# A hybrid encoder block on one core: the router's logits taken from sums ahead of the norm, the 64 greatest found in two halves, the first gather split, and one expert unit placed outside the weight ring

## The reference

```python
proj = h @ w_in                                    # z | xBC | dt | u | gate_a | gate_b
y_a  = ssd_branch(z, xBC, dt)                      # Mamba-2 scan in both directions, 24 heads
y_b  = s5_branch(u)                                # S5 scan in both directions, then GLU
mix  = sigmoid(gate_a) * y_a + sigmoid(gate_b) * y_b
h    = LN(alpha * h + mix @ w_o) * ln1_g + ln1_b
aff  = softmax(h @ w_router, axis=-1)              # 16 experts
gate, idx = top_k(aff.T, 64)                       # each expert takes the 64 tokens it likes best
xin  = h[idx]                                      # (16, 64, 1024)
hid  = silu(xin @ w_e1) * (xin @ w_e3)             # (16, 64, 2816)
moe  = scatter_add(idx, (hid @ w_e2) * gate)
out  = LN(alpha * h + moe) * ln2_g + ln2_b
```

## Time and profile before

| | |
|---|---|
| time, median of 3 runs | 2252.95 us (2252.62 to 2254.93) |
| profiled execution | 2250.3 us, its span 2248.3 us |
| PE busy | 1995.2 us, 89% of the span |
| DVE busy | 674.6 us, 30% |
| ACT busy | 328.2 us, 15% |
| POOL busy | 314.7 us, 14% |
| HBM traffic | 614.39 MB read, 9.78 MB written |

### The profile page before, as it was taken

How to read it: one execution, slowest core, us unless ns; L and a number is a source line. 1 busy time by engine, 2 the same in 40 slices (tenths; PEclk the granted TensorE clock), 3 DMA queues, 4 the chain that set the end, 5 groups by cost and what they waited for, 6 DMA issues and landing times.

```text
span 2248.3 us, 19706 instructions
## 1 busy us (share of the span) xinstructions
PE 1995.2 (89%) x8321; PEld 938.4 (42%) x8321; DVE 674.6 (30%) x1075; ACT 328.2 (15%) x547; POOL 314.7 (14%) x278
## 2 busy tenths in 40 slices
PE   8996899998979999598889889879889888988987
PEld 4664544455554444433334334334334333333332
DVE  6599965589970112300000000000000000000002
ACT  1433212144450001100000000000000000000001
POOL 2866600066640000000000000000000000000001
PEclk9898999999989999699999999999989999999999
DMA  5531221110013218389999999999999999999995
GB/s 138 126 107 26 66 96 69 39 52 28 29 57 131 84 66 351 122 341 427 429 428 424 428 428 425 431 426 427 429 427 427 428 426 427 428 427 426 427 428 228
DMA packets 86887, 625.45 MB, mean 278 GB/s; under 512 B 21036, under 2 KB 34576, under 8 KB 57616
## 3 DMA queue, kind: packets, MB, share of 16 engines
q1 hardware_dynamic: 74400, 616.41, 66.8%
q10 hardware_dynamic: 12400, 7.79, 1.2%
HBM read 614.39 MB, written 9.78 MB: 278 GB/s over the span
## 4 chain that ended last, share of the span: by engine, by line
PE 47%; DMA 28%; DVE 9%; ACT 2%; issue 1%; SPq 0%; DVEq 0%; ACTq 0%
PE ps L843 47%; DMA arena<-in_w_e 28%; ACT arena L568 1%; DVE arena L1598 1%; DVE arena L1546 1%; ACT L568 1%; DVE arena L1602 1%; DVE arena L1573 1%; DVE arena L1603 1%; DVE arena L1571 1%; DVE arena L1599 0%; DVE arena L1590 0%; DVE arena L1678 0%; DVE arena L1595 0%; DVE arena L1689 0%
## 5 line engine op out<-in xcount | busy, mean ns | idle before, releaser
L843 PE MATMUL ps<-arena 128*64 128x512 f32 (+7 forms) x7786 | 1927.6, 534 | 213.8 <-DMA arena<-in_w_e 114.5
L843 PEld LDWEIGHTS ps<-arena 128*64 128x64 f32 (+2 forms) x7786 | 877.4, 164 | 1247.8 <-issue 1062.5
L568 ACT ACTIVATE arena<-ps 128x512 f32<-128x512 f32 (+5 forms) x286 | 161.8, 597 | 1697.3 <-PE ps L843 898.2
L1698 DVE TENSOR_TENSOR arena<-arena,ps 128x512 f32<-128x512 f32 (+1 forms) x48 | 30.3, 645 | 581.5 <-PE ps L843 581.5
L560 POOL TENSOR_TENSOR arena<-arena 128x1024 f32<-128x1024 f32 x3 | 7.1, 2355 | 1324.8 <-ACT arena L568 1324.8
L1707 DVE TENSOR_TENSOR arena<-arena,ps 128x512 f32<-128x512 f32 x48 | 33.1, 690 | 338.5 <-PE ps L843 338.5
L568 ACT ACT_TABLE_LOAD x71 | 91.1, 1283 | 23.8 <-issue 21.4
L568 ACT ACTIVATE arena<-arena 64x512 f32<-64x512 f32 (+6 forms) x138 | 62.8, 513 | 164.2 <-DVE arena L1603 93.5
L1531 DVE SCALAR_TENSOR_TENSOR arena<-arena 128x512 f32<-128x512 f32 x80 | 62.5, 781 | 2.8
L1689 DVE TENSOR_TENSOR arena<-arena 128x512 f32<-128x512 f32 x8 | 5.6, 694 | 182.4 <-PE ps L1260 181.4
L544 POOL TENSOR_TENSOR arena<-arena 128x768 f32<-128x768 f32 x16 | 24.3, 1522 | 171.6 <-PE ps L1004 134.1
(11 more groups left out here) (180 smaller groups left out, 769.7 us busy)
## 6 DMA issues: line engine op xcount, KB each, us to landing
arena<-in_w_e SPq DMA_DIRECT2D x128, 2816.0 KB, 28.9
arena<-in_w_e SPq DMA_DIRECT2D x80, 2048.0 KB, 28.5
arena<-in_w_in SPq DMA_DIRECT2D x9, 2048.0 KB, 8.6
arena<-in_w_e SPq DMA_DIRECT2D x16, 1024.0 KB, 30.6
arena<-in_w_in SPq DMA_DIRECT2D x5, 1536.0 KB, 6.4
arena<-in_w_out_ssd SPq DMA_DIRECT2D x4, 1536.0 KB, 6.7
gate_scratch<-arena ACTq DMA_DIRECT2D x16, 256.0 KB, 2.4
arena<-gate_scratch SPq DMA_DIRECT2D x4, 1024.0 KB, 8.0
```

The source lines that it names most:

```text
L568: return act.activation(out, in_, func, **kw)
L843: return pe.matmul(out, lhsT, rhs, start=a, stop=z)
L1698: tt(o, o, ps[:, i, 0:w], ALU.mult).then_inc(s.hid_ready, 1)
```

## The change

- **Logits from the sums ahead of the norm.** Since h = (s - mean) / deviation * g + b with s = alpha x + mix @ w_o, the logits are (s @ (g w) - mean * sum(g w)) / deviation + sum(b w). So PE transposes `x_res` and multiplies it with the scaled router weights, and DVE corrects the result (`logits(c)`). The transposes and the router's matmuls of chunk c stand inside `out_product(c + 1)`. The scaled weights and the two rows of sums are made early: w_router is loaded behind slice 4 of w_in, POOL scales it twice, and PE and ACT make the two rows (`logit_rows`).
- **The 64 greatest in two halves.** `greatest(0)` works on chunks 0 and 1 between the two halves of the last output product, `greatest(1)` on chunks 2 and 3. The larger of the one's i-th and the other's (65 - i)-th value are the 64 greatest, and the least of them is a threshold. Slot numbers come from comparisons with the threshold and eight matmuls with triangles and ones.
- **The first gather in two parts.** Three of its eight blocks come ahead of `up(0, 0)`, five behind its first group.
- **Unit 7 aside.** It goes into the place of `x_res`, once h is finished (`h_ready` 4), and the ring holds the others. The order of release shifts: unit 8 now takes the place of unit 0.
- ln2_g and ln2_b are loaded behind the first pair's `up` instead of ahead of the search; ln1_g and ln1_b are read once more, as columns, with the early parameters.

The core of the diff:

```diff
@@ ring of expert weights: one unit's place lies outside it @@
-def ring_places(sizes, start, end):
+def ring_places(sizes, start, end, aside):
     for u, n in enumerate(sizes):
+        if u in aside:
+            places.append(aside[u])
+            behind.append(None)
+            continue
+        ASIDE = 7
+        unit_place, unit_behind = ring_places(unit_size, ring_at, WORDS, {ASIDE: aside_at})
@@ SP @@
             slices(0, FIRST_GATE + 1)
+            sp.dma_start(w_r[:, 0], A["w_router"][0].rearrange("(k p) e -> p k e", p=P)).then_inc(s.wr_loaded, 16)
...
-            sp.dma_start(w_r, A["w_router"][0].rearrange("(k p) e -> p k e", p=P)).then_inc(s.wr_loaded, 16)
...
-                if unit_place[u] + n_ > W0 - KT * EXPERTS and unit_behind[u] is None:
+                if u == ASIDE:
+                    sp.wait_ge(s.h_ready, TT)
+                elif unit_place[u] + n_ > W0 - router_words and unit_behind[u] is None:
                     sp.wait_ge(s.wo_ps, 2 * TT)
-                    sp.wait_ge(s.logit_ps, TT)
+                    sp.wait_ge(s.max_ready, TT)
@@ POOL @@
+            pool.wait_ge(s.par_ready, 1)
+            pool.wait_ge(s.wr_loaded, 16)
+            n.link(pool.tensor_tensor(w_r[:, 1], w_r[:, 0], last(ln1_cols[:, 1], EXPERTS), ALU.mult))
+            pool.tensor_tensor(w_r[:, 0], w_r[:, 0], last(ln1_cols[:, 0], EXPERTS), ALU.mult).then_inc(s.wr_scaled, 1)
+
             pool.wait_ge(s.rot_ready, 1)
             powers(fine, 0)
@@ ACT: ln1_g and ln1_b join the early parameters; later @@
+            act.wait_ge(s.rows_ps, 1)
+            n.done(f(logit_rows.rearrange("p r e -> p (r e)"), ps[:, 7, 0:2 * EXPERTS], ACT.Copy))
             act.wait_ge(s.seg_ps, 1)
...
+            for c in range(TT + 1):
+                if c < TT:
+                    mix_transposed(c)
+                if c >= 2:
+                    x_transposed(c - 2)
+                    exponents(c - 2)
+                if c >= 1:
+                    deviation(c - 1)
+            x_transposed(TT - 1)
+            exponents(TT - 1)
...
+                if p == 0:
+                    act.wait_ge(s.up_ps, 12)
+                    for i, name in enumerate(("ln2_g", "ln2_b")):
+                        act.dma_start(lnrow[:, i, :], A[name][0].partition_broadcast(P)).then_inc(s.ln_loaded, 16)
@@ PE @@
+            pe.wait_ge(s.wr_scaled, 1)
+            for k in range(KT):
+                r = mm(ps[:, 7, 0:2 * EXPERTS].rearrange("p (r e) -> p r e", r=2), ones, w_r[:, :, k, :], k == 0, k == KT - 1)
+            r.then_inc(s.rows_ps, 1)
...
+            mm(counts, m_le_l, over, True, False)
+            for c in range(1, TT):
+                mm(counts[:, c:], ones_l, over[:, 0:TT - c], False, False)
             for c in range(TT):
-                r = pe.transpose(ps[:, 4, EXPERTS * c:EXPERTS * c + EXPERTS], cum[:, P * c:P * c + P], ident[0:EXPERTS, 0:EXPERTS])
+                r = mm(counts[:, :, 1, :], ones_l, first(over[:, c, 0, :], TT), False, c == TT - 1)
             r.then_inc(s.slot_ps, 1)
...
                 for j in range(ROW_BLOCKS):
+                    if p == 0 and which == 0 and j == 1:
+                        first_gather(range(3, KT))
+                        pe.wait_ge(s.xin_copied, 2)
@@ DVE @@
+            def greatest(i):
+                dve.wait_ge(s.affT_ps, 2 * i + 2)
+                src = ps[0:EXPERTS, 2, 256 * i:256 * i + 256]
+                for r in range(CAP // 8):
+                    best = top64[:, i, 8 * r:8 * r + 8]
+                    n.link(dve.max(best, src))
+                    if r + 1 < CAP // 8:
+                        n.link(dve.match_replace(work, best, src, -1.0))
+                        src = work
...
             for c in range(TT):
+                residual(c, 0)
+                if c == TT - 1:
+                    greatest(0)
+                if c >= 1:
+                    logits(c - 1)
+                    affinities(c - 1)
+                residual(c, 1)
                 dve.wait_ge(s.wo_read, 2 * c + 2)
                 moments(x_res[:, c, :], c, s.var_ready)
                 dve.wait_ge(s.var_ready, c + 1)
+                deviation_inverse(c)
+                if c == TT - 1:
+                    logits(c)
                 centred(x_res[:, c, :], h[:, c, :], c)
...
+            affinities(TT - 1)
+            greatest(1)
+            n.link(tt(top64[:, 0], top64[:, 0], top64[:, 1, ::-1], ALU.max))
+            dve.tensor_reduce(threshold, top64[:, 0], AX.X, ALU.min).then_inc(s.threshold_ready, 1)
+            dve.wait_ge(s.threshold_ps, 1)
+            limit = first(ps[:, 5, 0:EXPERTS], TT)
+            tt(over[:, :, 0, :], aff, limit, ALU.is_gt).then_inc(s.over_ready, 1)
+            tt(over[:, :, 1, :], aff, limit, ALU.is_equal).then_inc(s.over_ready, 1)
+            normed(h[:, TT - 1, :], TT - 1).then_inc(s.h_ready, 1)
```

More of the change, by code:

```diff
@@ L206, in encoder @@
         ysT = H.take(S5_W // P, SEQ)
-        w_r = H.take(KT, EXPERTS)
+        w_r, logit_rows = H.take(2, KT, EXPERTS), H.take(2, EXPERTS)
         uT = ysT
@@ L295, in encoder @@
         xin = S.take(KT, P)
-        S3 = Space(arena, S.at, mix_end)
-        affT, work, cum = (S3.take(SEQ, parts=EXPERTS) for _ in range(3))
-        hid = S.take(FF)
         ye = hT.rearrange("p a b -> p (a b)")
@@ L1131, in mix_transposed, with out_product @@
                     r.then_inc(s.mixT_ps, 1)
-            def out_product(c):
+            def out_product(c, between, late):
                 pe.wait_ge(s.mixT_copied, 2 * (c + 1))
@@ L1143, in out_product @@
                         r = mm(ps[:, o_bank[c % 2][j], :], mixT[:, c % 2, k, :], w_o[j][:, k, :], k == 0, k == KT - 1)
+                        if c and j and k == 3:
+                            late(c - 1)
                     r.then_inc(s.wo_ps, 1)
-            def router(c):
-                pe.wait_ge(s.h_ready, c + 1)
-                for j in range(2):
-                    if 2 * c + j >= 1:
-                        pe.wait_ge(s.hT_copied, 2 * c + j)
-                    for k in range(4):
-                        kk = 4 * j + k
-                        r = pe.transpose(ps[:, 1, P * k:P * k + P], h[:, c, P * kk:P * kk + P], ident)
-                    r.then_inc(s.hT_ps, 1)
-                pe.wait_ge(s.hT_copied, 2 * (c + 1))
-                pe.wait_ge(s.wr_loaded, 16)
+                    if c and not j:
+                        between(c - 1)
@@ new lines, in x_transposed @@
+            def x_transposed(c, j):
+                pe.wait_ge(s.wo_read, 2 * c + j + 1)
+                if 2 * c + j >= 1:
+                    pe.wait_ge(s.hT_copied, 2 * c + (j if x_bank(c, j) else 0))
+                if not x_bank(c, j):
+                    pe.wait_ge(s.mixT_copied, 2 * TT)
+                for k in range(4):
+                    kk = 4 * j + k
+                    r = pe.transpose(ps[:, x_bank(c, j), P * k:P * k + P], x_res[:, c, P * kk:P * kk + P], ident)
+                r.then_inc(s.hT_ps, 1)
@@ L1166, in _, with between @@
+            def between(c):
+                if c == TT - 2:
+                    affinities_transposed(0)
+                    affinities_transposed(1)
+                x_transposed(c, 1)
+            for c in range(TT + 1):
                 if c < TT:
                     mix_transposed(c)
-                if 1 <= c <= TT:
-                    out_product(c - 1)
-            pe.wait_ge(s.aff_ready, 1)
-            for c in range(TT):
-                r = pe.transpose(ps[0:EXPERTS, 3, P * c:P * c + P], aff[:, c, :], ident)
@@ L1173, in _ @@
-            r.then_inc(s.affT_ps, 1)
-            pe.wait_ge(s.slotT_ready, 1)
-            for c in range(TT):
-                r = pe.transpose(ps[:, 4, EXPERTS * c:EXPERTS * c + EXPERTS], cum[:, P * c:P * c + P], ident[0:EXPERTS, 0:EXPERTS])
+                if c >= 2:
+                    x_transposed(c - 2, 0)
+                if c >= 1:
+                    out_product(c - 1, between, router)
+            x_transposed(TT - 1, 0)
+            x_transposed(TT - 1, 1)
+            router(TT - 1)
@@ new lines, in affinities @@
+            def affinities(c):
+                dve.wait_ge(s.rexp_done, c + 1)
+                n.link(dve.reciprocal(sm[:, 2, c:c + 1], sm[:, 1, c:c + 1]))
+                ts(aff[:, c, :], ex_t[:, c, :], sm[:, 2, c:c + 1], None, ALU.mult).then_inc(s.aff_ready, 1)
+            def greatest(i):
[7 more added lines that the diff above has]
+                        src = work
@@ L1667, in _ @@
-            n.done(dve.tensor_copy(logit, lg))
-            n.link(dve.tensor_reduce(sm[:, 0, :], lg, AX.X, ALU.max))
-            ts(sm[:, 1, :], sm[:, 0, :], -1.0, None, ALU.mult).then_inc(s.max_ready, 1)
-            dve.wait_ge(s.rexp_done, 1)
-            n.link(dve.reciprocal(sm[:, 3, :], sm[:, 2, :]))
-            tt(aff, ex_t, last(sm[:, 3, :], EXPERTS), ALU.mult).then_inc(s.aff_ready, 1)
-            dve.wait_ge(s.affT_copied, 1)
-            for r in range(CAP // 8):
```

(3 more changed lines are left out.)

167 lines of the change are left out of this document (104 added, 63 removed).

## The result

The changed kernel takes 2239.46 us (median of 5 runs, 2238.59 to 2241.81), the kernel before 2252.95 beside it: a ratio of 0.994, 95% interval 0.9926 to 0.9955. In a second measurement it was 2242.84 against 2252.51, 0.9948 (0.9934 to 0.9962). So the gain is 10 to 13.5 us, where 6.3 were forecast; the first measurement is about double the forecast. The profiled execution has a span of 2236.8 us against 2248.3, 11.5 us less, and these 11.5 can be laid out on the traces.

A forecast was written before the change was run, and what follows sets the result against it. Expert phase bound by DMA at 426 GB/s, S5 in front by DVE. From 2250.3 us, 20.3 gained behind and 14 lost in front give 2244.0 profiled; 2.65 more for the median makes 2246.6 us, range 2236 to 2256.

The forecast's parts named there:

- The front: Early part, where POOL waits for w_router before its powers: a loss of 14 us, bounds 5.7 and 25.
- `recur(0, 0)` starts 2.2 us late: DVE's first recur waits for POOL's first table, ready at 100.6 us: 2.2 us lost.
- 3.5 us as in that case, and ... 7.2: First recur lengthened by POOL's work beside it: 3.5 us from the second table, 7.2 from twelve map instructions.
- Behind: From the last output product through search, gather and expert phase: a gain of 20.3 us.
- step 1: Last output product ends at 910.9 us instead of 911.87, 1 us taken off; the first half's search is hidden.
- step 2: From the last output product to the logits: done at 917.7 us against 924.32; units 5 and 6 start there.
- Step 6: Unit 7 is loaded by group 0's use, so its 2.88 MB leave the DMA-bound phase: 6.7 us gained.
- Step 7: Five gather blocks behind group 0 delay release of units 10 and 11; DMA engines halt once: 1.8 us lost.
- Step 8: The two rows of ln2, 512 KB each, now load in the DMA-bound phase: 2.4 us lost.
- That the front costs nothing: Rival, 13%: DVE's instructions slip in between POOL's, only 2 us are lost in front: 2234.6 us.
- That the gain behind is smaller: Rival, 18%: PE stays at 1.2 GHz into groups 0 and 1; 13 to 15 us gained, 2251 to 2254 us.
- The slower one: Rival, 12%: late `block_diagonal(1)` stalls PE, gate products run at 1.2 GHz; front costs 25 us: 2257.7 us.

The follow-up runs named there:

- after_again: The changed kernel run once more, unedited, as control: 2242.84 us, 0.9948 of the kernel before.
- half_dose: scale_later with four unused memsets on POOL ahead of its powers: 2235.98 us, 0.9927 of the kernel before.
- scale_later: Changed kernel with POOL's router-weight products behind its last tables and PE's 16 small products behind the last xbc products: 2235.8 us, 0.9921 of before.
- wait_alone: scale_late, but POOL still waits for w_router at the old place ahead of its powers, computing nothing there: 2246.98 us, 0.9963 of before.
- long_dose: scale_later with fourteen unused memsets on POOL ahead of its powers: 2252.97 us, 0.9994 of the kernel before.
- scale_late: Changed kernel with POOL's router-weight products behind its last tables, PE's and ACT's parts in the xbc part: 2237.4 us, 0.9921 of before.

## Why the prediction was right, and where it was off

The verdict, the size of the gain behind and the place of the loss were right. The size of the whole was not: the sum was 5.2 us too cautious against the profiled execution (11.5 gained, 6.3 forecast), 4.6 of it in front and 0.6 behind, and 7.1 us against the median (2239.46 in place of 2246.6). The rest is that the median was taken as 2.65 us above the profiled execution, and it was 0.87.

**The front**, 14 us forecast, 9.4 measured. The mechanism was right; the step that failed is the one that sums up the first recur.
- POOL's powers were to start at 69.1. It was 65.94. The two more parameter loads shifted nothing (`par_ready` at 22.80, before 22.84), and w_router was in 9 us after its issue at 56.28, right behind slice 4, on which PE starts at 64.75.
- "`recur(0, 0)` starts 2.2 us late": in the profiled execution it did not, since the table came at 96.98 and PE's states at 98.39. In after_again the states came earlier and the table 0.8 us later, and the start was 2.1 us behind the states. So this term depends on when the states come, and that it was nothing here is partly luck. A delay of 23.3 us makes the start 8.6 us late.
- "3.5 us as in that case, and ... 7.2": the 10.7 us were 7.3, 2.3 for the table and 5.0 for the maps. The table's products began 1.3 us ahead of the recur, beside nothing of DVE's, so less of them met its later instructions than in recur(0, 1). The idea that each map product stops one instruction of DVE's for its whole 0.6 was wrong by a third: it was 0.42, and 0.43 in half_dose. The four products that read PSUM don't wait at all.
- PE's states late: 1 us forecast, 2.3 measured (30.1 against 27.8 from recur(0, 1) to (1, 0)).
- 7.3 + 2.3, less the 0.7 that comes back, is 8.9, and 0.5 comes in SSD and the mixing, where two executions of one program are further apart than that.

The Trainium skill, "SBUF — State Buffer", section "Who interferes with whom", has a VectorE instruction with two on-chip inputs contend with a GpSimd instruction that reads on-chip memory, and one with at most one such input not, and calls the port pair that they share an exclusive lock. The traces agree as to which instructions suffer: 0.69 for those with an input in PSUM, 1.37 or 0.78 for scans. They don't show that one waits out the other whole. Alone, scans start every 0.32 us and the map products take 0.60 each, which would make 0.92 a pair one after the other; beside each other a scan starts every 0.70 us (105.64, 106.34, 107.05, 107.75). The 21.1 us that the prediction drew from the rule for recur(0, 0) are 17.7.

**Behind**, 20.3 forecast, 20.9 measured. Shifted by the front's 9.4, the steps stood at 920.3, 937.6, 942.4, 947.7 and 957.2 for the last product, the comparisons, `sel`, the first group and its use; they were at 918.8, 935.25, 940.35, 945.6 and 955.37. The difference is made by the last product, 1.5 us in step 1, and by the logits, 0.9 in step 2; from there every step came within half a us of its length. Both have to do with the clock. Step 1 left out that the 16 router matmuls ahead of the last product ran in part at the lower level before: the product takes 13.7 of the 17.47 us of the earlier trace rows, so these took 3.7, and at full clock they take 1.96.

```profile
894.00:902.00 8.00, 7.60 (x26) 4.59 (x27) 2.94 (x4) 0.55 (x2) 0.00 (x0) 0.79 0.00 0
```

In the changed kernel the last product runs at 1.00, and in all 13 profiles with the new order it ends 67.6 us behind M, before 70.1. Step 2, from the product's end to the issue of unit 5, was put at 6.8 us and took 6.0: ACT's copies ended 0.4 us sooner, and the router, forecast at the lower level and 2.1 us behind them, ran at 1.00 and ended 1.5 us behind them. That is partly luck. In scale_later the clock falls ahead of the same instructions, and the step takes 7.65 us.

So the 17.8 became 19.65. Step 6 (6.7) was 6.5 to 6.9. Step 7's halt of 1.8 is there and is larger: units 10 and 11 go out 15.75 us behind 8 and 9 (15.4 forecast), which leaves 2.3 over the 13.5 of a transfer, and unit 10 lands 9.3 us behind unit 9 where units in one go land 6.7 apart, 2.6 more. Step 8's 2.4 was 2.4 to 2.9 at the landing of the last weights. With 2.6 for each of the last two, 19.65 + 6.8 - 2.6 - 2.6 is 21.3, and the last weights do land 21.8 us earlier behind M than before (1359.9 us, not 1381.6). The last landing is 24.9 us ahead of the end before and 25.8 after, which takes 0.9 off and leaves the 20.9. So that the sum came within 0.6 is in part errors that cancel.

**The rivals.** That the front costs nothing is out (wait_alone). That the gain behind is smaller is out: PE's clock was 1.2 GHz only from 924 to 945 us (0.52) and 2.4 GHz through groups 0 and 1 (0.98, 1.00). The slower one asked for a front loss of 24.8 us. Its mechanism, PE standing behind `block_diagonal(1)`, exists (10.07 us of waiting, then two gate products in 17.86 us in place of 13.7), but DVE, busy with its own work until 143.9, hid all but 2.2 of it. Not even long_dose, with PE waiting 20.4 us for ACT, lost more than 17.5.

## What to carry to other kernels

An in-order engine's idle time is a cover only for what it does next: a wait for a load, put ahead of work that was ready, cost 9 us here, though the engine had been idle for 38 us ahead of that work. Put it behind the first work that is long enough to hide the landing: between the two `powers` it costs some half a us (262.6 us to C, 262.1 before). And when an engine is late, look not only at who waits for it but at what it will now run beside: of the 9.6 us that were lost by the start of recur(1, 0), 7.3 were VectorE instructions that nobody delayed, only lengthened.

## What the hardware showed unexpectedly

- The loss from VectorE and GpSimd running side by side grew with the length of the partner's instructions in the two lengths that occur here: a scan of 0.40 us takes 0.78 beside products of 128x256, 1.37 beside products of 128x512, and those with an input in PSUM 0.69 in either case.
- The last of ACT's DMA issues at the start takes 2.8 to 6.7 us where its neighbours take 0.46, and ACT's first exponential stands behind it, so that `rot_ready` came between 52.8 and 57.2 us in executions of kernels that are the same up to there. In nine of the thirteen that issue it from ACT, `rot_ready` starts 30.8 us behind the end of that issue. scale_late's 55.0 is not explained by it: its issue took 2.98 us, and PE's clock from 13 to 18 us was 0.66, where the changed kernel has 1.00. This is the timeline of ACT in scale_later:

```profile
19.10 0.47 ACTq L620 DMA_DIRECT2D arena<-in_s_b_re  x1
19.60 6.74 ACTq L620 DMA_DIRECT2D arena<-in_s_b_im  x1
26.37 1.28 ACT L595 ACT_TABLE_LOAD   x1 [26.37 <-issue]
```

- The clock falls at different places in executions with the same work, and that moves single us. The last chunk's router, 16 small instructions, took 1.96 us in the changed kernel, with the clock at 1.00 from 921.9 to 924 us (2.4 GHz), and 3.59 in scale_later, with 0.50 from 919.4 to 923 (1.2 GHz). Two executions of the changed kernel took 200.1 and 203.2 us over SSD, and 25.8 and 27.4 us behind the last weights.
